# Weight-sum transfers issued step by step over all runs of weights, in a hybrid attention / RWKV-7 layer

## The reference, cut to what matters

```python
h = rmsnorm(x); proj = h @ w_in          # q,k,v | RWKV-7 features | two gate blocks
att = sliding_window_attention(q, k, v)
rw, S = rwkv7_mix(p_rw, shift, S0)       # a recurrence over the tokens
x = x + (sigmoid(g0) * (att @ w_branch[0]) + sigmoid(g1) * (rw @ w_branch[1])) @ w_out
h2 = rmsnorm(x)
x = x + (silu(h2 @ w_ffn_gate) * (h2 @ w_ffn_up)) @ w_ffn_down     # 1024 -> 2816 -> 1024
```

## Time and profile before

| | |
|---|---|
| runs | 3108.81 us median of 3 (3107.2 to 3109.02) |
| profiled execution | 3109.36 us, its span in the trace 3107.3 us |
| TensorE | busy 3073.3 us, 99% of the span |
| DMA queue q1 (issued by SP) | 537.02 MB, 53.1% of 16 engines over the span |
| DMA queue q0 (issued by POOL: the weight sums) | 37.75 MB, 5.5% of 16 engines over the span |

### The profile page before, as it was taken

The page is one execution under the profiler, slowest core; times in us unless marked ns, Lnnn a source line. Parts: engine busy times, 40 slices in busy tenths (PEclk is TensorE's granted clock), DMA queues, the critical chain, the costliest instruction groups (busy, mean ns, idle before and its releaser), DMA issues.

```text
span 3107.3 us, 66192 instructions
## 1 busy us (share of the span) xinstructions
PE 3073.3 (99%) x27589; PEld 2614.2 (84%) x27589; DVE 1771.0 (57%) x3064; ACT 1110.4 (36%) x2039; POOL 345.0 (11%) x333
## 2 busy tenths in 40 slices
PE   8999999999999999999999999999999999999998
PEld 6877878888888788888888788998888879999998
DVE  6565645457776768355565466313666644565555
ACT  5544433334444444332333144313333322322222
POOL 0011110001111100010221000001122110022111
PEclk9999999999999999999999999999999999999999
DMA  5476565237666676255566673267566576476665
GB/s 184 159 243 207 164 200 184 95 109 247 199 215 222 217 250 213 95 168 159 184 179 206 181 237 124 90 197 221 178 178 175 173 205 193 144 236 224 218 222 164
DMA packets 291207, 579.48 MB, mean 186 GB/s; under 512 B 37344, under 2 KB 40800, under 8 KB 289888
## 3 DMA queue, kind: packets, MB, share of 16 engines
q1 hardware_dynamic: 276896, 537.02, 53.1%
q0 software_dynamic: 13440, 37.75, 5.5%
q10 hardware_dynamic: 576, 0.49, 0.1%
HBM read 463.16 MB, written 149.83 MB: 197 GB/s over the span
## 4 chain that ended last, share of the span: by engine, by line
PE 95%; DVE 2%; ACT 1%; DMA 1%; issue 1%; SPq 0%; POOL 0%; DVEq 0%; POOLq 0%; ACTq 0%
PE PS L1060 76%; PE PS L1131 6%; PE PS L1078 6%; PE PS L1190 1%; PE PS L1256 1%; DMA wl<-weight_lo 1%; PE PS L1430 1%; PE PS L1240 1%; PE PS L1180 1%; PE PS L1437 0%; PE PS L1216 0%; PE PS L1226 0%; PE PS L1124 0%; PE PS L1125 0%; DMA raw<-w 0%
## 5 line engine op out<-in xcount | busy, mean ns | idle before, releaser
L1060 PE MATMUL PS<-hh,wh 128*128 128x512 f32 x1864 | 749.6, 402 | 1.6 <-DMA wl<-weight_lo 1.4
L1060 PE MATMUL PS<-hh,wl 128*128 128x512 f32 x1864 | 727.6, 390 | 0.0
L1060 PE MATMUL PS<-hl,wh 128*128 128x512 f32 x1864 | 726.9, 390 | 0.0
L1474 ACT ACTIVATE wh<-raw 128x512 fp32r<-128x512 f32 x452 | 283.7, 630 | 418.3 <-PE PS L1060 348.4
L1993 DVE TENSOR_TENSOR wl<-raw,wh 128x512 fp32r<-128x512 f32 x452 | 321.4, 713 | 183.5 <-ACT wh L1474 180.4
L1060 PEld LDWEIGHTS PS<-hh,wh 128*128 128x128 f32 x1864 | 349.8, 188 | 83.0 <-issue 3.0
L1060 PEld LDWEIGHTS PS<-hh,wl 128*128 128x128 f32 x1864 | 349.8, 188 | 75.7
L1060 PEld LDWEIGHTS PS<-hl,wh 128*128 128x128 f32 x1864 | 350.4, 188 | 68.4 <-issue 1.0
L1060 PE MATMUL PS<-fh,wh 128*128 128x512 f32 x528 | 213.4, 404 | 3.0 <-DMA wl<-weight_lo 3.0
L1060 PE MATMUL PS<-fh,wl 128*128 128x512 f32 x528 | 206.1, 390 | 0.0
L1060 PE MATMUL PS<-fl,wh 128*128 128x512 f32 x528 | 205.9, 390 | 0.0
(11 more groups left out here) (373 smaller groups left out, 5788.7 us busy)
## 6 DMA issues: line engine op xcount, KB each, us to landing
wh<-weight_hi SPq DMA_DIRECT2D x470, 256.0 KB, 2.8
wl<-weight_lo SPq DMA_DIRECT2D x470, 256.0 KB, 3.5
raw<-w SPq DMA_DIRECT2D x176, 512.0 KB, 3.6
weight_hi<-wh SPq DMA_DIRECT2D x164, 256.0 KB, 4.4
weight_lo<-wl SPq DMA_DIRECT2D x164, 256.0 KB, 4.7
raw<-w SPq DMA_DIRECT2D x96, 256.0 KB, 3.1
weight_sums<-w POOLq DMA_DIRECT2D x24, 1024.0 KB, 10.3
sf<-weight_sums SPq DMA_DIRECT2D x72, 256.0 KB, 4.5
```

Source lines behind the costliest of these rows:

```text
L1060: mm = pe.matmul(PS[:, bank(t) + f, 0:t.cols], wt[:, cols], mov[:, m, (t.half + f) * t.cols:(t.half + f + 1) * t.cols], start=(first and a ...
L1474: act.activation(wh[h % 4][:], src, ACT.Copy).then_inc(hi_done, 1)
```

## The change

The 40 transfers are issued in another order: step by step over all five runs, instead of run by run over all eight steps. Sum 1 is begun with the quarter (0, 0) of `w` and sum 0 is then added to it, where before sum 0 was copied into it and the quarter added; sum 2 likewise with sum 1. So the ten transfers that read sums become accumulating DMAs, and ten that read `w` become plain copies. A transfer that adds waits for all five first transfers of its sum (`R`), one that reads a sum for all ten of it. The tags put 10 transfers into F1 (50 quanta apart), 10 into A3 (14 quanta apart, from `Q["A", 3] + 8`) and 20 into F2.

```diff
-        SUM_STEPS = ((0, (1, 0)), (3, (0, 0)), (0, (1, 1)), (3, (1, 0)), (1, 0), (1, (0, 0)), (2, 1), (2, (0, 1)))
+        SUM_STEPS = ((0, (1, 0)), (3, (0, 0)), (0, (1, 1)), (3, (1, 0)), (1, (0, 0)), (1, 0), (2, (0, 1)), (2, 1))
 
         def sums_tag(i):
-            b, i = divmod(i, 4 * len(SUM_RUNS))
-            return Q["F", b + 1] + 6.0 + 464.0 / (4 * len(SUM_RUNS)) * i
+            early, mid, n = 2 * len(SUM_RUNS), 4 * len(SUM_RUNS), 8 * len(SUM_RUNS)
+            if i < early:
+                return Q["F", 1] + 10.0 + 500.0 / early * i
+            if i < mid:
+                return Q["A", 3] + 8.0 + 14.0 * (i - early)
+            return Q["F", 2] + 10.0 + 460.0 / (n - mid) * (i - mid)
...
             def weight_sums():
-                for i, ((s, js), (u, source)) in enumerate(itertools.product(SUM_RUNS, SUM_STEPS)):
+                R = 16 * len(SUM_RUNS)
+                for i, ((step, (u, source)), (s, js)) in enumerate(itertools.product(enumerate(SUM_STEPS), SUM_RUNS)):
                     yield sums_tag(i)
                     n0, g = SEVENS.index(js[0]), len(js)
                     out = summed[:, u, n0:n0 + g, :]
-                    done = 2 * (i // 8)
-                    if i >= 2:
-                        pool.wait_ge(s_made[u], 16 * (done + sum(1 for v, _ in SUM_STEPS[:i % 8] if v == u)))
+                    adds = any(v == u for v, _ in SUM_STEPS[:step])
+                    if adds:
+                        pool.wait_ge(s_made[u], R)
                     if isinstance(source, int):
-                        pool.wait_ge(s_made[source], 16 * (done + 2))
-                        pool.dma_start(out, summed[:, source, n0:n0 + g, :]).then_inc(s_made[u], 16)
+                        pool.wait_ge(s_made[source], 2 * R)
+                        pool.dma_start(out, summed[:, source, n0:n0 + g, :], accum_op=ALU.add).then_inc(s_made[u], 16)
                         continue
...
-                    if any(v == u for v, _ in SUM_STEPS[:i % 8]):
+                    if adds:
                         pool.dma_start(out, part, accum_op=ALU.add).then_inc(s_made[u], 16)
```

## The result

The changed kernel takes 3139.1 us (median of four runs, 3138.23 to 3139.3) against 3108.2 us before: the ratio is 1.0097, 95% interval 1.0085 to 1.0109. It is slower by 31 us; 3132 us (3111 to 3150) was forecast, slower with a chance of 0.81.

The account below looks back on a forecast made before the run. TensorE, with 95% of the chain, was taken to bound the kernel. On the profiled 3109.4 us, +24 - 2.5 - 1.0 + 3 = +23.5 gave 3132.9, 3132 by the median; range 3111 to 3150 us.

Parts of the forecast that it names:

- That the ten leave POOL in a row at the end of F1: Ten adds tagged for A3 leave POOL one after another from about 1801 us, since nothing on POOL waits there.
- How long the burst lasts, and what it leaves to the loads: End of F1 and B2: 4752 packets at 66.5 in a microsecond, 71.5 us, with as many packets for the loads.
- The term of 24 us: End of F1 and B2: loads fall 33.5 us behind, less 9 us of cover; TensorE loses 24 us, between 7 and 33.5.
- 9 us of cover: End of F1 and B2: buffers give a `wl` load about 9 us to spare, the same taken for raw loads.
- a falling clock as a rival: In the burst the waiting array falls to half clock, up to 22 us more, 3154 us; chance 0.03.
- What TensorE would wait for: In the burst at F1's end and B2, TensorE waits for DMA or for `wh`/`wl`, some 20 us in all.
- F1: A bunch of a copy and two adds becomes two copies, so its waits go: -2.5 us, between 1.9 and 3.0 gained.
- F2's start: Two waits at 2157 and 2161 shrink as a copy replaces an add: -1.0 us, between 0 and -1.4.
- the cap on the gain: Whole kernel: TensorE's waits for DMA, four for `wl` in F1 and F2, limit any gain to 4.4 us, 0.14%.
- F2's end: Three adds from `weight_sums` run together, priced nearer to adds from `w` than to the copy: +3 us, between 0 and 11.
- where their tags say: Rival: the ten run in A3, 10.5 us apart, and only the gains are left, 3106 us; chance 0.08.
- drains like copies: Rival: queued adds in the burst cost like copies, 37 us for the row, 3109.5 us in all; chance 0.13.

Follow-up runs that it names:

- hold_a3: Changed kernel with each of the ten A3 transfers made to wait until TensorE reaches the quantum of its tag: 3110.8 us, ratio to before 1.0006.
- copies: Changed kernel with the ten transfers as plain copies in place of adds, in the same row at the same place: 3122.2 us, one run.
- half_burst: Changed kernel with only the first five of the ten adds leaving in a row, the other five held to their tags in A3: 3122.8 us, one run.
- hold_w2: Changed kernel with all ten adds still in one row, but only once TensorE reaches the first quantum of W2: 3112.2 us, one run.
- x_later: Changed kernel with the last block's loads of x, their squares and what follows up to the rounded planes 20 quanta later: 3136.9 us, one run.
- all_in_a: Changed kernel with all 40 transfers held by waits on TensorE's progress to stages A1 (15), A2 (10) and A3 (15): 3108.1 us, ratio 0.9998.
- small_a3: hold_a3 with the five adds of sum 1 into sum 2 issued as 18, packets 2 KB and not 8 KB: 3104.6 us, ratio to before 0.9986.

## Why the prediction was right, and where its sizes were off

*That the ten leave POOL in a row at the end of F1* was right to within the shift of that time (1797.17 against "about 1801"), and so was the reason: hold_a3 changes nothing but the moment of issue, and the 28.1 us are gone.

*How long the burst lasts, and what it leaves to the loads* was right. The step said packet for packet, 66.5 of each in a microsecond, for 71.5 us. The queues of the changed kernel from 1797 to 1862:

```profile
q0 software_dynamic: 4368, 8.65, 72.7%
q1 hardware_dynamic: 4314, 7.65, 36.4%
```

That is 67 and 66 in a microsecond, and q0 has its last packets before 1872, as forecast. The runs copies, half_burst and hold_w2 agree with it: fewer packets in the row, or fewer wanted beside it, and the loss falls or goes.

*The term of 24 us* measured 28.1, and that it came so near is in part luck. TensorE's idle time is 8.3 + 16.0 = 24.3 us, the number forecast; but the forecast reached it by taking 9 us of cover from 33.5, and the two shorter rows show no such cover. By the forecast's own count the copies put the loads 11.5 us behind, and half the row, 2376 packets, 35.7 - 24.4 = 11.3 us. With 9 us of cover they would have cost 2.5 and 2.3 us; they cost 11.8 and 10.3. So the loss is close to what the loads fall behind, and the cover, read from a single load's delay, was sized too large. Why a load's own slack does not carry over to a whole row was not tested.

The clock was left out of the term, too. Of the 28.1 us 23.9 are idle time that was not there before (the kernel before waits 0.4 us for `e` in B2), and 2.2 are the clock: after the 16 us wait eleven matmuls follow at the lower level, 0.43 us apart in place of 0.23 (11 x 0.2). The other 2 us are not accounted for. The forecast kept a falling clock as a rival at 0.03 because F1's window showed 1.00, but F1's waits were of 1.6 us at most; a single wait of 16 us is another thing. The Trainium skill ("TensorE: Matmul & The Clock Gate", section "Part 1: The HAM clock gate") has the idle array fall to 1.2 GHz, and here the trace agrees: 0.50.

*What TensorE would wait for* was only half right. In F1's end it is `wl`, as said. In B2 it is not a raw load but the evacuation `e` on DVE. The chain of the changed kernel there, in order of time (start, us, what):

```profile
1840.99 20.43 DMA xin<-x
1861.42 0.02 issue
1861.44 0.67 ACT nt L1637
1862.11 0.02 issue
1862.13 0.06 DVE nsum L2320
1862.19 0.58 issue
1862.77 0.69 DVE acc L2126
1863.46 0.03 issue
1863.49 0.05 DVEq L2113
1863.54 0.05 issue
1863.60 0.70 DVE e L2118
```

A load of x that took 20.4 us held ACT's square, this DVE's sum, and behind that stood the evacuation whose bank TensorE needed. In x_later, with x 20 quanta later, the longest wait begins 18 us later, again behind x, and is 11.8 us long; what TensorE would have waited for without that order is not shown.

*F1*, -2.5, measured -2.6 from F1's first `kk` to `leadmu` (1362.61 to 1796.16, 433.5 us; before from 1363.56 to the 1799.70 of the earlier trace rows, 436.1). That is the good end of what this code does: in eight of the nine other runs with the same transfers in F1, one wait for `wl` of 1.4 to 1.8 us is left near 1740, and F1 takes 434.2 to 434.7 us, 1.5 to 2 less than before. *F2's start*, -1.0, measured -2.1 over F2 up to its last `kk`, outside its bounds of 0 and -1.4; no wait is left in it, but the two that went were 1.4 us together, and the other 0.7 is not accounted for. So the cap on the gain, the 4.4 us of waits, was a little low as well: in all_in_a F1 and F2 together are 5.5 us shorter.

*F2's end* was mis-sized: +3, measured +6.6, inside the bounds of 0 and 11. The step that failed is "being adds they are nearer to the second": by time the add from `weight_sums` is (41.9% of 13 us from 2299 on in the changed kernel, 5.4 us a MB, between 3.0 and 6.9), but it keeps the 144 packets of the copy, and the share of the loads goes by packets. In the changed kernel, from 2545 to 2555:

```profile
q0 software_dynamic: 256, 1.84, 88.1%
q1 hardware_dynamic: 257, 0.49, 14.7%
```

One for one again, but each of q0's is 7 KB and q1 gets 49 GB/s; beside adds from `w` it got 0.49 MB in 4 us. That is the upper bound's mechanism, and small_a3 shows it. Idle time is 3.8 of the 6.6 us; the granted clock, 0.77 and then 0.89 over the 20 us from 2550, is part of the rest.

So the 29.0 us of the spans are the forecast's 23.5 with 4 more for B2, 3.5 more for F2's end, and 2 less for F1 and F2. The "where their tags say" rival is refuted by the trace, the "drains like copies" one by the packets counted.

## What to carry to other kernels

A tag, a due time or a place in program order paces a DMA only as far as the instructions around it wait: before moving transfers into a stage, look what else the issuing engine does there, and if that is nothing, hold them with a wait on the progress of the work that they are to run beside. A background transfer is not priced by its bytes. While its queue is busy, the loads get one packet for each of its own, so its price is how far that puts the loads behind what they want in that time: here 1 MB adds of 2 KB packets cost nothing in A3, where the loads kept the engines at 0.34, and 28 us at the end of F1 and in B2. For the same bytes small packets leave the loads more: cutting 7 KB packets into 2 KB ones turned a 3.9 us wait into none. With both mended the change is worth 4 us, 0.14%.

## What the runs showed of the hardware that was not expected

- Two busy DMA queues share one for one in packets whatever their size (266:266, 719:719 and 4368:4314 at 2 KB, 256:257 at 7 KB against 1.9 KB).
- SP's issue slows down beside POOL's row: six loads of x took it 9.85 us from 1840.52 in the changed kernel, and 2.81 us from 1833.65 before. Busy engines alone do not do it, for before the change q1 took 98.5% of them at that time; what holds the issue is not shown.
- The granted clock fell to 0.50 in one wait of 16 us and to 0.84 (over 10 us) behind one of 3.9 us in hold_a3, while it stayed at 1.00 through the seven waits of up to 1.6 us from 1800 to 1840.
